# The corner loads of a delta-rule scan, issued from ScalarE instead of SyncE

## What is computed

```python
def gdn_scan(q, k, v, g, beta, S0, return_y):
    ...
    decay = jnp.exp(jnp.where(incl, gcum[..., :, None] - gcum[..., None, :], -jnp.inf))
    kk = jnp.einsum('bchik,bchjk->bchij', k_beta, kc) * decay
    tmat = (jnp.eye(Q, dtype=jnp.float32) + jnp.where(strict, kk, 0.0)).astype(jnp.float32)
    rhs = jnp.concatenate([vc * bc, k_beta * jnp.exp(gcum)[..., None]], axis=-1).astype(jnp.float32)
    sol = lax.linalg.triangular_solve(tmat, rhs, left_side=True, lower=True, unit_diagonal=True)
    ...
    def step(S, inp):
        u_i, w_i, kd_i, d_i = inp[:4]
        v_new = u_i - jnp.einsum('bhqk,bhkv->bhqv', w_i, S)
        S_next = S * d_i[..., None, None] + jnp.einsum('bhqk,bhqv->bhkv', kd_i, v_new)
        ...
        o = jnp.einsum('bhqk,bhkv->bhqv', qd_i, S) + jnp.einsum('bhij,bhjv->bhiv', qk_i, v_new)
        return S_next, o
```

## Time and profile before

| | us |
|---|---|
| median of three runs | 2649.74 |
| lowest, highest | 2648.49, 2650.87 |
| the profiled execution | 2649.97 |
| its span, first to last instruction | 2648.1 |
| TensorE busy | 2456.2 (93%) |
| VectorE busy | 1405.5 (53%) |
| ScalarE busy | 1021.7 (39%) |

### The profile page before, as it was taken

How to read it: one execution, slowest core, us unless ns; L and a number is a source line. 1 busy time by engine, 2 the same in 40 slices (tenths; PEclk the granted TensorE clock), 3 DMA queues, 4 the chain that set the end, 5 groups by cost and what they waited for, 6 DMA issues and landing times.

```text
span 2648.1 us, 30258 instructions
## 1 busy us (share of the span) xinstructions
PE 2456.2 (93%) x11894; PEld 1970.4 (74%) x11894; DVE 1405.5 (53%) x2280; ACT 1021.7 (39%) x1687; POOL 152.8 (6%) x116
## 2 busy tenths in 40 slices
PE   3899999889789889999999899999999899999997
PEld 2788878634479877788887767888888767888886
DVE  8567765488836453544445554444445454444445
ACT  3445458422232273422335354322224444422222
POOL 0000000000000001000003301000002210100002
PEclk9999999855599999999999999999999999999998
DMA  5233425411132232222232211232223210222222
GB/s 230 104 120 120 159 96 182 150 19 36 57 104 74 80 136 88 89 96 96 96 99 93 65 38 33 96 101 97 96 94 104 68 45 24 96 96 98 101 96 80
DMA packets 124445, 248.28 MB, mean 94 GB/s; under 512 B 58064, under 2 KB 58832, under 8 KB 123536
## 3 DMA queue, kind: packets, MB, share of 16 engines
q1 hardware_dynamic: 119728, 236.38, 27.2%
q10 hardware_dynamic: 4576, 9.96, 1.0%
HBM read 221.13 MB, written 25.17 MB: 93 GB/s over the span
## 4 chain that ended last, share of the span: by engine, by line
PE 78%; DVE 8%; SPq 4%; ACT 3%; DMA 3%; issue 3%; POOL 0%; DVEq 0%; ACTq 0%
PE bank L1217 17%; PE bank L1219 17%; PE bank L1218 17%; PE bank L929 4%; PE bank L1080 3%; PE bank L1377 2%; PE bank L1368 2%; DVE cacc L2000 1%; PE bank L1067 1%; DMA raw<-in_s_qkvx 1%; PE bank L928 1%; PE bank L392 1%; PE bank L393 1%; PE bank L394 1%; SPq L764 1%
## 5 line engine op out<-in xcount | busy, mean ns | idle before, releaser
L1664 ACT ACTIVATE whi<-raw 128x1024 fp32r<-128x1024 f32 (+1 forms) x267 | 277.7, 1041 | 927.9 <-PE bank L1219 923.2
L1217 PE MATMUL bank<-ahi,whi 128*128 128x512 f32 x1152 | 454.7, 395 | 9.0 <-DVE alo L2388 6.0
L1219 PE MATMUL bank<-ahi,wlo 128*128 128x512 f32 x1152 | 450.7, 391 | 0.0
L1218 PE MATMUL bank<-alo,whi 128*128 128x512 f32 x1152 | 450.6, 391 | 0.0
L2270 DVE TENSOR_TENSOR wlo<-raw,whi 128x1024 fp32r<-128x1024 f32 (+1 forms) x267 | 327.4, 1226 | 135.1 <-ACT whi L1664 134.7
L1217 PE MATMUL bank<-bhi,whi 128*128 128x512 f32 x736 | 286.6, 389 | 0.0
L1219 PE MATMUL bank<-bhi,wlo 128*128 128x512 f32 x736 | 286.3, 389 | 0.0
L1218 PE MATMUL bank<-blo,whi 128*128 128x512 f32 x736 | 286.3, 389 | 0.0
L1217 PEld LDWEIGHTS bank<-ahi,whi 128*128 128x128 f32 x1152 | 217.8, 189 | 59.5 <-issue 10.6
L1218 PEld LDWEIGHTS bank<-alo,whi 128*128 128x128 f32 x1152 | 217.9, 189 | 46.1 <-issue 1.4
L1219 PEld LDWEIGHTS bank<-ahi,wlo 128*128 128x128 f32 x1152 | 217.6, 189 | 45.6
(11 more groups left out here) (417 smaller groups left out, 4088.2 us busy)
## 6 DMA issues: line engine op xcount, KB each, us to landing
raw<-in_s_gu SPq DMA_DIRECT2D x88, 512.0 KB, 3.3
raw<-in_s_qkvx SPq DMA_DIRECT2D x34, 512.0 KB, 4.9
late_modw<-in_w_mod SPq DMA_DIRECT2D x32, 512.0 KB, 3.5
raw<-in_s_up SPq DMA_DIRECT2D x32, 512.0 KB, 3.2
raw<-in_s_down SPq DMA_DIRECT2D x32, 512.0 KB, 3.3
raw<-in_s_dn SPq DMA_DIRECT2D x32, 512.0 KB, 3.3
raw<-in_s_win SPq DMA_DIRECT2D x24, 512.0 KB, 3.3
raw<-in_s_zg SPq DMA_DIRECT2D x16, 512.0 KB, 4.0
```

The lines of the kernel that those rows point to most:

```text
L1217: pe.matmul(out, w_hi, x_hi, start=start, stop=False)
L1218: pe.matmul(out, w_hi, x_lo, start=False, stop=False)
L1219: return pe.matmul(out, w_lo, x_hi, start=False, stop=stop)
L1664: act.activation(whi[u % 2][:, 0:width[u + 2] * P], raw[u % 2][:, 0:width[u + 2] * P], ACT.Identity).then_inc(hi_ready, 1)
```

## The change

load_corners moves from SyncE's list to ScalarE's. The three transfers of a quarter and what they add to pre_loaded stay the same; 72 transfers (six steps, four quarters, three each) are concerned. On ScalarE they stand

- for step 0 ahead of the first PM copies, behind waits for the stores of AT (at_stored) and for the zeroing of C5 and C6 (zeroed);
- for step 1 behind each PM copy of corner6 of step 0, quarter by quarter;
- for steps 2 to 5 behind all four PM copies of corner6 of the step before.

No wait for p6_full is written for them: the PM copy ahead of them has waited for it.

```diff
@@ -763,15 +763,6 @@
-            def load_corners(t, q):
-
-                d, m = q // 2, at_dram[pair_of(q, t)]
-                for src, dst in ((0, 1), (2, 3)) if d == 0 else ((1, 0), (3, 2)):
-                    part = lambda x: x[32 * src:32 * src + 32, :].rearrange("i (j n) -> i j n", j=4)[:, :, 32 * dst:32 * dst + 32]
-                    sp_.dma_start(part(C5[q][:, :]), part(m)).then_inc(pre_loaded[q], 16)
-                half = lambda x: x[64 * d:64 * d + 64, :].rearrange("i (j n) -> i j n", j=4)[:, :, 64 - 64 * d:128 - 64 * d]
-                sp_.dma_start(half(C6[q][:, :]), half(m)).then_inc(pre_loaded[q], 16)
-
...
             for q in range(4):
                 load_d32(0, q)
-                sp_.wait_ge(zeroed, 4 + 2 * (q + 1))
-                load_corners(0, q)
...
                     load_d32(t, q)
-                    load_corners(t, q)
@@ -1664,6 +1652,20 @@
             split(JOB["wout"].u0 - 1)
+            def load_corners(t, q):
...
+                    act.dma_start(part(C5[q][:, :]), part(m)).then_inc(pre_loaded[q], 16)
...
+                act.dma_start(half(C6[q][:, :]), half(m)).then_inc(pre_loaded[q], 16)
+
+            for s in range(4):
+                act.wait_ge(at_stored[s], 16 * 6)
+            for q in range(4):
+                act.wait_ge(zeroed, 4 + 2 * (q + 1))
+                load_corners(0, q)
             act.wait_ge(xb_stored, 48)
             act.wait_ge(xv_stored, 48)
...
             for q in range(4):
                 corner(0, q, p6_full)
+                load_corners(1, q)
...
                 if more:
                     for q in range(4):
                         corner(t + 1, q, p6_full)
+                if t + 2 < NCH:
+                    for q in range(4):
+                        load_corners(t + 2, q)
                 if t == 0:
```

More of the change, by code:

```diff
@@ L1666, in _ @@
             split(JOB["wout"].u0 - 1)
+            def load_corners(t, q):
+                d, m = q // 2, at_dram[pair_of(q, t)]
+                for src, dst in ((0, 1), (2, 3)) if d == 0 else ((1, 0), (3, 2)):
+                    part = lambda x: x[32 * src:32 * src + 32, :].rearrange("i (j n) -> i j n", j=4)[:, :, 32 * dst:32 * dst + 32]
+                    act.dma_start(part(C5[q][:, :]), part(m)).then_inc(pre_loaded[q], 16)
+                half = lambda x: x[64 * d:64 * d + 64, :].rearrange("i (j n) -> i j n", j=4)[:, :, 64 - 64 * d:128 - 64 * d]
+                act.dma_start(half(C6[q][:, :]), half(m)).then_inc(pre_loaded[q], 16)
[4 more added lines that the diff above has]
+                load_corners(0, q)
             act.wait_ge(xb_stored, 48)
```

## The result

| | before | after |
|---|---|---|
| median, us | 2650.3 (4 runs, 2648.49 to 2651.9) | 2613.7 (4 runs, 2613.06 to 2615.52) |
| the profiled execution, us | 2649.97 | 2615.52 |
| its span, us | 2648.1 | 2613.7 |
| TensorE's waits for C or DB in the scan, us | 30.7 | 8.0 |

The ratio after / before is 0.9858, with a 95% interval of 0.9843 to 0.9873: 36.6 us off, where 30.7 had been forecast.

The account below looks back on a forecast made before the run. The prediction took the scan to be bound, for part of each step, by SyncE's rate of issuing small transfers. Gains of 25.6 (later steps) and 5.1 us (scan's start), 30.7 off 2649.97, gave 2619.3 us; range 2613 to 2638.

Parts of the forecast that it names:

- Bound and cause: Scan: for part of each step bound by SyncE's rate of issuing small transfers, not bandwidth; TensorE waits 30.7 us for C5/C6.
- the second term of Part 4: Step 0 of the scan: the wait before the fourth corner product goes, worth 2.16 us.
- Part 4: Start of the scan: 6.76 us of waits go, loads between PM copies cost 1.65 us; net 5.1 us gained.
- Part 2: Corner loads on ScalarE: 0.63 us an issue, each transfer there 1.5 to 3 us before TensorE wants it.
- The shared generator: Rival: one descriptor generator for both queues, 1.1 us per corner issue on ScalarE; 2630 to 2640 us, chance 0.15.
- Part 1: SyncE after the move: 28 issues a step, 13.3 us; data landed 8.5 us after the last second corner product (X).
- SyncE's quarter takes 3.4 us: Sign that the forecast is right: SyncE's issues for one quarter of a step take 3.4 us.
- The forecast's slack of 4.6 us: Each late step: SyncE's data landed at 8.5 us after X, wanted by TensorE at 13.1.
- SyncE stays last: Rival: SyncE's 28 issues stretch to 0.8 us each, waits nearly stay; 2645 to 2650 us, chance 0.07 including otherwise no change.
- Part 3: Steps 1 to 5 of the scan: vanished waits, priced start to start, give 10.5, 3.65, 6.0 and 5.45, together 25.6 us.
- small-shift case of 2617: Start of the scan: clock rises sooner after 722 us, up to 2 us more gained; within 2614 to 2626, chance 0.69.
- more than that: Whole kernel: a gain larger than the forecast with its small shifts; chance 0.03.

Follow-up runs that it names:

- The repeat: The changed kernel itself measured once more, nothing altered: 2615.05 us, ratio 0.9868 to before.
- y_first: Changed kernel with the 2 MB store of y issued on ScalarE's queue ahead of step 2's corner loads: 2621.91 us, ratio 0.9891 to before.
- warm: Changed kernel with eight useless 128x512 matmuls (warming products) ahead of the first corner product: 2621.95 us, ratio 0.9882 to before.
- zs_late: Changed kernel with the 2 MB load of zs, and the work needing it, behind step 0's corner loads: 2613.31 us, ratio 0.9851 to before.
- grouped: Changed kernel with step 1's twelve corner loads behind all four PM copies of step 0, not between them: 2614.83 us, ratio 0.9863 to before.
- warm_y_late: Changed kernel with eight useless matmuls before the first corner product and the store of y one stage later: 2614.3 us, ratio 0.9857 to before.

## Where the prediction was right, and where it failed

**Bound and cause: right.** Waits for C behind SyncE's issues bound the scan; taking the issues away took the waits away, and more issues on either queue brought them back. The step that failed is the second term of Part 4: the wait before step 0's fourth corner product was put at its own 2.16 us, and its going gave 4.6, since the low clock behind the wait went with it. The direction and the mechanism were right, the gain was too small: 30.7 us against 36.6.

**Part 2, the cost on ScalarE: right.** 0.63 us an issue was taken; a quarter of three takes 1.96 us, so 0.65. In step 1 the last corner product stands at 776.05, which is 11.57 us behind X (764.48); 11.6 was forecast, with no wait. The PM copies of step 0 start 1.8 to 2.0 us apart (732.40, 734.17, 736.13, 738.10), 2.0 forecast. The shared generator, as a rival at 1.1 us an issue that would have cost 17 to 21 us, is refuted by the rows above. The Trainium skill (Perfetto Trace Analysis, DMA Instruction — HWDGE) says that one instruction holds the generator for itself, and also that the profiled duration contains the wait for it. So durations that overlap don't speak against the rule, and the forecast's rival read it too strictly when it added the two durations up. That SyncE's issues for DB grow from 0.43 us to 0.61 while ScalarE issues agrees with it, but no run here isolates it.

**Part 1, what SyncE has left: wrong by 3 us, without effect.** Its data was to be there 8.5 us behind X. In the step shown above X is 826.65; the last piece is issued until 836.3, so 9.7 behind X and not 6.6, and has landed at about 11.2, with 13.1 wanted. The 28 issues take 16.1 us (820.18 to 836.32), 0.58 each, gaps included; the sum used 0.475 from a burst alone. The sign "SyncE's quarter takes 3.4 us" therefore failed while ScalarE issues (4.25), and holds where it doesn't (3.3 from 855.54 to 858.86). The forecast's slack of 4.6 us was 1.8. It held, but the forecast did not know how near it was; halving DB's loads showed it. "SyncE stays last" was nearer than its 0.07 says.

**Part 3, the later steps: right to 0.1 us.** Forecast 25.6. From the first state update to the scan's end it was 940.82 - 765.26 = 175.56 us before, and is 907.22 - 757.33 = 149.89: 25.67 less. By steps it is 10.54, 3.65, 6.04 and 5.44, where 10.5, 3.65, 6.0 and 5.45 were forecast. Reading start-to-start distances against an undisturbed group price, and not the wait rows, is what made this exact, since it carried the lost clock with it. It is exact against the one trace that it was read from; that another execution of a kernel that waits can differ by 2 us, the trace with step 0's loads alone shows.

**Part 4, the scan's start: too small, 5.1 forecast and 7.5 measured.** Its terms, from the earlier trace rows, the rows above and two rows more of the kernel before, the first corner products and the second ones:

```profile
721.83 4.94 PE L1080 MATMUL bank<-DB,C 128*128 128x128 f32 x24 [7.08 <-DMA C<-at_scratch]
...
735.12 3.74 PE L1080 MATMUL bank<-DB,C 128*128 128x128 f32 x32
```

| | forecast | measured |
|---|---|---|
| first corner product, against the scan's start | 0 | -0.9 (11.9 us behind it before, 12.8 after) |
| from there to the second corner product | 2.16, and "up to 2" for the clock as a small shift | 4.6 (13.29 to 8.71) |
| on to step 1's first corner product | -1.65 | -1.5 (7.14 to 8.62) |
| step 1's corner products, first to fourth | 4.60 | 5.3 (14.86 to 9.55) |
| sum | 5.1 | 7.5 |

The failing term is the second: 2.16 forecast, 4.6 measured. The other 2.4 us are the low clock: the four first corner products take 8.58 us from start to the next block before, 2.16 of it the wait, and 5.14 after; the block products behind them take 4.71 before and 3.57 after. That the clock is what such a block costs, the warming products show: at full clock the first corner products take 3.99 us. The text had the rising clock as a small shift to be added, not in the sum, though the profile of before shows the clock at 0.56 between 731 and 733, behind the wait that was going to go. Part 3 counted the clock that a vanished wait gives back; Part 4 did not. The last line is the same mistake in small: it summed wait rows (0.57, 1.63, 2.40) where distances were to be had, which give 5.3.

**What stays open.** Part 4's miss is 2.4 us of the 5.9 between the 30.7 forecast and the 36.6 measured. The scan is 33.3 us shorter: 25.7, and 7.6 up to the first state update. The other 3.3 us between the medians are 0.35 ahead of the scan, 0.8 behind it, and 2.2 between profiled executions and medians, and no run here shows their cause. The stretch behind the scan lies between 1706.5 and 1708.7 us in the traces of this document, so its 0.8 can't be told from scatter. The 2.2 may lie in the kernel before, whose profiled execution, 2649.97 us, is below the median of each of its four batches (2650.3 to 2652.0). The repeat gave 36.0 between medians. The forecast's small-shift case of 2617 was the nearest; more than that had been given 0.03 only, and the lower end of the range, 2613, left no room for a gain of 37 us.

## What to carry to other kernels

When an engine waits on a chain of small transfers, count issues, not bytes: here each cost 0.43 to 0.65 us, halved or whole, and a second queue that issued beside the first took SyncE's part of a step from 21.3 us to 16.1. Price a vanished wait by start-to-start distances against an undisturbed stretch, at every place alike, for the clock that it gives back belongs to it. After such a move, work out the slack of both queues anew, and look where a big transfer stands in order to the small ones of the other queue: a fraction of a microsecond of order can cost seven of time.

## What was not expected of the hardware

A 2 MB transfer in flight slows small ones of the other queue in two ways: their landing went from 2 us to 7.1 and 7.8 (y_first, warm), and their issue from 0.43 to 0.62 us up to 1.87, for several issues in a row on both queues (y_first). A single slow issue is not proof of it: in the changed kernel one of SyncE's took 2.22 us and one of ScalarE's 1.72 at 766 us, with only small loads under way (74 GB/s), and no run shows why.

An issue's price did not follow its size: half a corner piece took the same 0.63 us as a whole one.

The time before the scan scatters more than the scan: the last yfm copy lies between 707.6 and 713.2 us in the profiled executions here, and the scan of the changed kernel repeats within 0.3 us, where the scan of a kernel that waits may differ by 2. So a change of a microsecond or two in this scan can be read in a trace, but not in the medians of four or five runs; that is why the orders of zs_late, grouped, warm_y_late and the changed kernel stay open.
